# A two-layer encoder trunk with routed experts: residual inside the first expert, counts behind the selection, norm per token tile, each attention query one pair later

## The reference

```python
for l in range(2):
    sh1, sc1, g1, sh2, sc2, g2 = split(silu(c) @ w_ada[l] + b_ada[l], 6)
    h = x * (1 + sc1) + sh1
    if l == 0: y = conformer_conv(h, ...)      # 2 projections, 31 taps, norm
    else:                                      # k, v, forget gates from x;
        y = fox_attention(h @ w_q, k, v, fcum) @ w_o     # 16 heads of 64, causal
    x = layer_norm(ALPHA * x + (1 + g1) * y, ln_mix_g[l], ln_mix_b[l])
    h = x * (1 + sc2) + sh2
    probs = softmax(h @ router_w + router_b)   # group by its best two, then top 2
    y = sum over the chosen e of weight * ((silu(h @ w_gate[l,e]) * (h @ w_up[l,e])) @ w_down[l,e])
    x = layer_norm(ALPHA * x + (1 + g2) * y, ln_ffn_g[l], ln_ffn_b[l])
```

## Time and profile before

| | |
|---|---|
| timed runs | 1350.45 us median of 3 (1350.08 to 1356.78) |
| profiled execution | 1354.81 us, span 1353.1 us |
| mean granted TensorE clock | 0.923 |
| TensorE matmul | 1102.8 us busy (82%), 13118 instructions |
| VectorE, ScalarE, GpSimd | 430.4 (32%), 169.1 (12%), 21.1 us (2%) |
| DMA | 494.74 MB, mean 366 GB/s |
| chain that ended last | PE 56%, DMA 36%, DVE 4%, ACT 2%, issue 2% |

### The profile page before, as it was taken

The page is one execution under the profiler, slowest core; times in us unless marked ns, Lnnn a source line. Parts: engine busy times, 40 slices in busy tenths (PEclk is TensorE's granted clock), DMA queues, the critical chain, the costliest instruction groups (busy, mean ns, idle before and its releaser), DMA issues.

```text
span 1353.1 us, 30933 instructions
## 1 busy us (share of the span) xinstructions
PE 1102.8 (82%) x13118; PEld 653.6 (48%) x13118; DVE 430.4 (32%) x1378; ACT 169.1 (12%) x411; POOL 21.1 (2%) x61
## 2 busy tenths in 40 slices
PE   4999989669997689666999979695699996796666
PEld 2885345335554245333575853562356663453333
DVE  0697252113332123111472332431133231231114
ACT  1113130001010001000201420300010110000001
POOL 1300000000000000000000000000000000000000
PEclk9899979889999899888999989598899998998888
DMA  9985599999999999999995433789999899999990
GB/s 356 385 319 226 226 426 422 425 423 425 426 426 423 426 424 424 425 425 422 414 414 231 173 125 134 302 361 422 424 427 426 337 411 424 425 425 424 424 413 37
DMA packets 56959, 494.74 MB, mean 366 GB/s; under 512 B 4196, under 2 KB 12420, under 8 KB 17176
## 3 DMA queue, kind: packets, MB, share of 16 engines
q1 hardware_dynamic: 55920, 490.75, 87.5%
q10 hardware_dynamic: 744, 2.35, 0.5%
q0 software_dynamic: 192, 0.15, 0.0%
HBM read 492.19 MB, written 1.05 MB: 365 GB/s over the span
## 4 chain that ended last, share of the span: by engine, by line
PE 56%; DMA 36%; DVE 4%; ACT 2%; issue 2%; SPq 0%; DVEq 0%; POOLq 0%
PE PS L1079 24%; DMA ring<-in_w_up_dram 21%; DMA ring<-in_w_gate_dram 8%; PE PS L977 6%; PE PS L1201 4%; DMA ring<-in_w_down_dram 3%; PE PS L1107 3%; PE PS L884 3%; DMA work<-in_w_gate_dram 2%; PE PS L1058 2%; PE PS L994 2%; PE PS L1325 2%; DMA ring<-in_w_ada_dram 2%; PE PS L1070 1%; PE PS L1372 1%
## 5 line engine op out<-in xcount | busy, mean ns | idle before, releaser
L1079 PE MATMUL PS<-ring,work 128*32 128x256 f32 x8160 | 519.7, 411 | 171.7 <-DMA ring<-in_w_up_dram 71.6
L1079 PEld LDWEIGHTS PS<-ring,work 128*32 128x32 f32 x8160 | 282.7, 117 | 393.9 <-issue 121.2
L1641 DVE TENSOR_TENSOR work<-work,PS 128x256 f32<-128x256 f32 x47 | 19.8, 422 | 452.9 <-PE PS L1079 452.9
L977 PE MATMUL PS<-ring,work 128*128 128x512 f32 x192 | 83.4, 594 | 0.5 <-ACT work L818 0.5
L686 ACT ACTIVATE work<-PS 128x256 f32<-128x256 f32 x47 | 18.0, 383 | 449.8 <-PE PS L1079 449.8
L1079 PE MATMUL PS<-work 128*32 128x256 f32 x864 | 54.5, 394 | 16.9 <-DMA work<-in_w_gate_dram 8.5
L884 PE MATMUL PS<-ring,cact 128*32 128x512 f32 x384 | 50.3, 662 | 16.5 <-DMA ring<-in_w_ada_dram 16.5
L1201 PE MATMUL PS<-work,ring 128*128 128x256 f32 x256 | 58.1, 390 | 2.2 <-ACT work L623 2.2
L1058 PE MATMUL PS<-hs,work 128*32 128x256 f32 x784 | 56.2, 406 | 3.8 <-DVE work L1609 3.8
L1107 PE MATMUL PS<-work 32*128 32x256 f32 x784 | 56.2, 400 | 3.8 <-DVE work L1654 3.8
L977 PEld LDWEIGHTS PS<-ring,work 128*128 128x128 f32 x192 | 36.3, 190 | 46.4 <-issue 45.6
(11 more groups left out here) (254 smaller groups left out, 881.9 us busy)
## 6 DMA issues: line engine op xcount, KB each, us to landing
ring<-in_w_gate_dram SPq DMA_DIRECT2D x58, 2048.0 KB, 34.1
ring<-in_w_up_dram SPq DMA_DIRECT2D x58, 2048.0 KB, 34.9
ring<-in_w_down_dram SPq DMA_DIRECT2D x58, 2048.0 KB, 28.0
ring<-in_w_ada_dram SPq DMA_DIRECT2D x24, 2048.0 KB, 20.8
work<-in_w_up_dram SPq DMA_DIRECT2D x6, 2048.0 KB, 19.4
work<-in_w_gate_dram SPq DMA_DIRECT2D x6, 2048.0 KB, 34.1
work<-in_w_down_dram SPq DMA_DIRECT2D x6, 2048.0 KB, 42.5
ring<-in_w_pw_dram SPq DMA_DIRECT2D x8, 1024.0 KB, 12.1
```

The lines of the kernel that those rows point to most:

```text
L977: last = pe.matmul(PS[:, banks + 2 * t + q, :], moving[:, k, t * P:(t + 1) * P], quarter(index + h, kk, KH)[:, q * BANK:(q + 1) * BANK], s ...
L1079: last = pe.matmul(dst[SLOTS * s:SLOTS * (s + 1), :], rows[:, cc, SLOTS * q:SLOTS * (q + 1)], quarter(load + h, kk, KH)[:, QUART * s:QUART ...
```

## The change

- `residual` moves, in both layers, to between the hidden loop and the result loop of expert 0. `rT`'s first two chunks are scaled ahead of ScalarE's logit copy, the other six where all eight were; a Silu on one column follows them.
- In layer 0, two of the four ada loads of the K/V rows stand ahead of the counts and two behind, in PSUM bank 0 in place of bank 4.
- The mix norm: each engine normalizes its half of tile 0 and then of tile 1, with a semaphore for each tile. All transposes go tile by tile, not bank by bank.
- `hT` has a semaphore for each copying engine; the first convolution projection and the first query wait for pairs of chunks.
- The loop of pairs runs `query(i+1)` from round 1 in place of `query(i+2)` from round 0.
- The norm rows' two halves lie in different strips (partitions 72 on and 104 on), filled by eight DMAs in place of four.

```diff
+    NORM_ROWS = (NORM_ROW, NORM_ROW + 32)
-        ROWS = 16 * 7
+        ROWS = 16 * 11
             for n, w in enumerate((ln_mix_g, ln_mix_b, ln_ffn_g, ln_ffn_b)):
-                load_rows(NORM_ROW + 4 * n, w.rearrange("l (h n) -> (l h) n", n=BANK))
+                for h in range(2):
+                    load_rows(NORM_ROWS[h] + 2 * n, w[:, h * BANK:(h + 1) * BANK])
...
             def spread_ln(n, l, bank):
-                spread_row(lambda i: NORM_ROW + 4 * n + 2 * l + i, bank)
+                spread_row(lambda i: NORM_ROWS[i] + 2 * n + l, bank)
...
-                    act.activation(chunks(hs, 1)[:, 1], by_chunk(xs[:, 1, :])[:, 1], ACT.Identity, bias=negm[:, 1:2],
-                                   scale=rstd[:, 1:2]).then_inc(n_half, 1)
+                    for t in range(TT):
+                        act.activation(chunks(hs, t)[:, 1], by_chunk(xs[:, t, :])[:, 1], ACT.Identity, bias=negm[:, t:t + 1],
+                                       scale=rstd[:, t:t + 1]).then_inc(n_half, 1)
...
+                residual_T(range(2), rT_begun)
                 act.wait_ge(logits_parted, 2 * l + 1)
                 act.activation(parts[:, 0, :], PS[:, B_GATE, 0:SEQ], ACT.Copy).then_inc(parts_kept, 1)
                 act.wait_ge(lmax_ready, l + 1)
                 act.activation(r_ex[:, :, :], r_ex[:, :, :], ACT.Exp).then_inc(lexp_ready, 1)
-                for k in range(KD):
-                    last = act.activation(rT[:, k, :], ...)
-                last.then_inc(rT_ready, 1)
+                residual_T(range(2, KD), rT_ready)
+                act.activation(warm[:, :], cact[:, 0:1], ACT.Silu)
...
-                if i + Q_AHEAD < PAIRS:
-                    take_q(i + Q_AHEAD)
+                if 1 <= i < PAIRS - 1:
+                    take_q(i + 1)
...
+            def turn_h(chunk, norms=None):
+                for t in range(TT):
+                    if norms is not None:
+                        of_sums = norms % 2 == 0
+                        pe.wait_ge(h_ready, TT * (norms - 1) + (TT if of_sums else t + 1))
+                        pe.wait_ge(n_half, TT * (norms - 1) + (TT if of_sums else t + 1))
+                    for k in range(KD):
+                        last = pe.transpose(PS[:, k // 2, ...], chunk(t, k), ident[:, :])
+                        if t == TT - 1 and k % 2 == 1:
+                            last.then_inc(h_turned, 1)
-            def h_there():
-                pe.wait_ge(hT_copied, 4 * hs_turned[0])
+            def h_there(k):
+                by = (hT_by_act, hT_by_dve)[k // 2 % 2]
+                pe.wait_ge(by, 2 * hs_turned[0] - 1 + k // KH)
...
                 if l == 0:
-                    for j in range(ADA_G - 1):
-                        ada_load(L_ADAKV, j, B_GATE)
-                else:
-                    residual()
+                    pe.wait_ge(rT_begun, 1)
+                    for j in range(2):
+                        ada_load(L_ADAKV, j, 0)
...
                 if l == 0:
-                    ada_load(L_ADAKV, ADA_G - 1, B_GATE)
-                    residual()
+                    for j in range(2, ADA_G):
+                        ada_load(L_ADAKV, j, 0)
...
-                if l == 0:
-                    pe.wait_ge(ada_added, 4)
                     with pe.Fori(0, blocks):
                         hidden_of(pe.snap(n_pe) + 1, index + 6 * e)
+                    if e == 0:
+                        if l == 0:
+                            pe.wait_ge(ada_added, 4)
+                        residual()
                     with pe.Fori(0, blocks):
                         result_of(pe.snap(m_pe) + 1, index + 6 * e)
...
+                        if f == g == 0 and k % 2 == 0:
+                            h_there(k)
...
-                    dve.tensor_scalar(chunks(hs, 1)[:, 0], by_chunk(xs[:, 1, :])[:, 0], ...)
-                    dve.tensor_scalar(chunks(hs, 0), by_chunk(xs[:, 0, :]), ...).then_inc(h_ready, 1)
+                    for t in range(TT):
+                        dve.tensor_scalar(chunks(hs, t)[:, 0], by_chunk(xs[:, t, :])[:, 0], ...).then_inc(h_ready, 1)
```

More of the change, by code:

```diff
@@ L670, in moe, with residual_T @@
             def moe(l):
+                def residual_T(chunks_of, done):
+                    for k in chunks_of:
+                        last = act.activation(rT[:, k, :], PS[:, k // 2, (k % 2) * SEQ:(k % 2 + 1) * SEQ], ACT.Identity,
+                                              bias=rescol[:, 2 + l, k:k + 1], scale=rescol[:, l, k:k + 1])
+                    last.then_inc(done, 1)
+                residual_T(range(2), rT_begun)
                 act.wait_ge(logits_parted, 2 * l + 1)
@@ L818, in take_o @@
                 act.activation(QT[:, i, :], PS[:, i % 2, 0:SEQ], ACT.Copy).then_inc(o_copied, 1)
-            for i in range(Q_AHEAD):
+            for i in range(2):
                 take_q(i)
@@ L1188, in _ @@
                     for j in range(4):
-                        last = pe.matmul(PS[:, 5, 16 * j:16 * (j + 1)], rows[:, j:BANK:4], ident[:, NORM_ROW:NORM_ROW + 16],
-                                         start=True, stop=True, skip_group_check=True)
+                        of_norms = ident[:, :].rearrange("p (q r) -> p q r", q=4)[:, 2:4, NORM_ROW % 32:NORM_ROW % 32 + 8]
+                        last = pe.matmul(PS[:, 5, 16 * j:16 * (j + 1)].rearrange("p (h v) -> p h v", h=2), rows[:, j:BANK:4],
+                                         of_norms, start=True, stop=True, skip_group_check=True)
                         if j == 0:
@@ L1324, in query @@
                         arrived(L_WQ + k // KH)
+                    if i == 0 and k % 2 == 0:
+                        h_there(k)
+                        if k == 0:
+                            h_there(2)
                     last = pe.matmul(PS[:, (i + 1) % 2, SEQ:2 * SEQ],
```

62 lines of the change are left out of this document (25 added, 37 removed).

## The result

In the first comparison the changed kernel took 1340.39 us (median of 7 runs, 1338.26 to 1343.67), the kernel before beside it 1355.08 (7 runs, 1349.97 to 1356.78): ratio 0.9912, interval 0.9891 to 0.9934, which is 0.9% or 11.9 us less [8.9, 14.8]; the two medians lie 14.7 apart. A second comparison gave 1339.54 and 1355.14: 0.9885 [0.9854, 0.9915]. The time lies in the forecast's range, 2.2 us over its number. The profiled executions have spans of 1341.3 and 1341.0, against 1353.1 and, in a second profile taken later, 1356.0 before.

What follows compares the result with a forecast made beforehand. The weight stream bounds the kernel, so savings pay only before 159 us, from 631 to 883 us and in the tail. Terms -0.7 - 1.6 - 4.0 + 0.4 - 6.4 sum to -12.3: 1338.2 us from 1350.45, range 1334 to 1343.5.

Steps and rivals of the forecast that it cites:

- Per-pair waits, -0.7: First convolution projection: starting after two chunks per copying engine, 0.95 us earlier, saves 0.7 us, bounds 0.4 and 1.0.
- Strips, -1.6: Between the K halves: spread matmuls reading different row strips take 2.1 us at most, saving 1.6, bounds 1.2 and 1.8.
- Query one pair later, -4.0: Attention pair loop: query(7) fills round 6, removing a 2.67 us stall plus 1.3 of clock loss; bounds 0 and -4.4.
- Norm per token tile, +0.4: Layer 1's mix norm: scale and shift come later, so hT's copies end later, costing 0.4 us; bounds -0.2 and +1.0.
- Residual out of the routing, -6.4: Layer 1's routing: counts start at 862.5 instead of 868.87, saving 6.4 us; bounds -5.5 and -6.8.
- Residual into the first expert, 0: Layer 1's first expert: the first down slot is released later, but 3.9 us are to spare; cost 0, bounds 0 and +6.
- (1): Attention gives nothing: a softmax stall at the pair loop's head replaces the one removed at its tail; 1342.2 us, chance 0.12.
- (2): TensorE stays at half clock from the routing through layer 1's first expert, leaving 4.7 us of gain; 1345.7, chance 0.06.
- (3): The attention pair loop becomes softmax-bound in every round, losing 7.7 us overall; 1358.2 us, chance 0.03.
- (4): The start gives nothing or loses because the small norm-row DMAs land late; 1339 to 1341 us, chance 0.06.
- the forecast's tests: Wrong if the second expert stage lengthens by over 2 us, or time before 631 us changes by over 1.5.

## Why the prediction was right, and where it was off

- *The base.* The sum was -12.3 from the profiled execution, 1354.81, which gives 1342.5, and from the median shown, 1350.45, which gives 1338.2. The later medians of before are 1355.08 to 1356.33. So the three runs shown were on the fast side and the profiled one was typical; the measured differences are 11.9 (14.7 between the medians) and 15.6. The mechanism of most terms held, but that 1338.2 came within 2.2 us is partly luck: the base was 4.6 too low and the sum too small, and the two errors lie on opposite sides. From 1355.08 the same sum gives 1342.8.
- *Per-pair waits, -0.7.* The first projection starts 0.8 us sooner behind the copies (forecast 0.95). But from the third ada product to the end of "conv" almost nothing is left: with that product at full clock 128.81 before and 128.66 to 128.87 in the three kernels that had it so (query, residual and norm undone); at half clock 130.27 before and 130.19 on average in the eight with the waits per pair. Where the product was as long as before's 3.27 (3.24, both waits filled) it is 129.79, half a us less. The matmuls moved forward ran at half clock, and it came back later after the first projection: 42 to 44 us has 0.91 in before's second profile (first projection 37.90) and 0.78 in the changed kernel's first (37.46). So the edit was worth 0 to 0.5 against before, 0.1 by the mean, and not 0.7. Taking it back cost 0.6 to 1.3 in the one profile there is; that the two disagree is open. At the first query the forecast's 0 holds. The query starts 0.37 sooner (3.16 to 2.79 us from the transposes' start), but the gates' matmuls behind it now wait 0.32 for VectorE, and the second query stands 5.01 us behind the first, not 4.64. Putting the wait back costs 0.5 net (0.9 in "K/V" less 0.4 in "pairs"), more than against before, since transposing tile by tile fills the first bank later.
- *Strips, -1.6.* The spread gave 1.71. But "K/V" fell by 3.77: 0.37 is the query's wait, which "pairs" takes back, and 1.69 is the K half behind the spread, 15.70 for 14.01 in both profiles of before and never in the eleven with the fast spread. With the strips undone the clock fell elsewhere in that stage and cost 1.5. So each of the three profiles with the slow spread lost 1.5 to 1.7 us to the clock in this stage and none of the eleven others did; why, no run shows. With that the term was -3.4, about twice the forecast and outside its bounds.
- *Query one pair later, -4.0 (bounds 0 and -4.4).* "pairs" fell from 71.76 to 67.5 or 69.8: -4.3 or -1.9, and 0.37 more if the gates' wait is left out. Exactly the one wait of 2.67 went. The clock part did not come as foreseen: the fall did not go with the wait, it moved behind the next one in all nine profiles, and how long it lasts decides. Undoing the edit, with one short fall on either side, gave 3.3. That -4.0 came so near to -4.3 is luck: in both profiles of before the clock fell twice, which in the kernel with the edit undone it did not. The head of the loop had less to spare than the forecast 0.8: diagonals ready 750.42, turn at 750.64.
- *Norm per token tile, +0.4.* Undoing it gave 0.41 in its one profile, with the transposes at full clock in both (1.97 and 2.10 us). Against before's profiles it looks like -0.2, because in both of these part of the transposes was at half clock (2.65 us for 1.97).
- *Residual out of the routing, -6.4.* "wait" 6.48 to 0.05. "sums" is 10.4 in all that have no fill, as said. The forecast has no term for "select", which fell from 9.68 to 8.45 and 8.81 because the clock fell later, nor for "out", 1.0 longer in the first profile, where the clock of "pairs" was still down.
- *Residual into the first expert, 0, with 3.9 us to spare.* The cover measures 4.3 to 4.5 in the profiles, about 6 by the medians.
- *Rivals.* No stall at the head (1); the first expert rose to full clock within its hidden strips (0.71 in 870 to 874, 1.00 behind) (2); rounds 1 to 6 don't wait (3); the start didn't lose (4).

The terms as measured in the stages, -0.1 - 3.8 - 1.9 or -4.3 - 0.2 - 6.4, make -12.4 or -14.8. With "select" (-1.2, -0.9) and "out" (+1.0, 0), and without the first term, which stands earlier, these are the 12.5 and 15.5 us between 210.9 and 198.4 or 195.4. Of these some 10.4 are the waits and the spread (6.4, 2.7 and 1.7, less 0.4 in the norm). The other 2.1 or 5.1 are the clock, which stood lower in both profiles of before behind the spread, in "select" and, against the second profile of the changed kernel, in "pairs"; the forecast had 1.3 for it. Of the forecast's tests, "rest" holds. The time before 631 us holds on average: the first K matmul is at 668.32 and 669.65 before, and at 666.60 to 670.33, mean 668.4, in the eleven profiles with the first edit. In the changed kernel's own two profiles it is 1.8 and 2.0 later than in before's first, over the 1.5 allowed, and 0.5 and 0.7 later than in before's second; the stream-paced "experts 0" has two levels there, 508.0 to 508.6 and 510.5 to 510.9, that no edit here sorts. So that an edit of layer 0 gave or cost something in it can't be told.

## What to carry to other kernels

Work that depends on nothing near it goes where the bottleneck engine is waiting for data or the stream is ahead, not between a selection and its consumer; size the cover by adding work until the stage grows. Count with every slow or idle stretch of TensorE the microseconds at half clock that follow it, and compare stages only between profiles in which the clock stood alike. Take the base of a forecast from as many executions as there are: here the median of three runs was nearly 5 us off, more than any single term but one.

## What the runs showed of the chip

- Four 32-row matmuls between two strips took 1.92 us, from one strip 3.63. Only in the three profiles with the slow form did TensorE fall to 1.2 GHz in the K/V stage: in two within 8 us behind it, though it was busy throughout, and in one 45 us later.
- At the end of the first wait of 2.67 us in the pair loop, or within 2 us behind it, the granted clock fell to 0.50 in all twelve profiles with such a wait. It came back and stayed in eight, came back and fell again behind the second wait in both of before, and stayed at 0.50 through the second wait in two; in the two profiles with the waits filled it never fell.
- TensorE at half clock in the routing rose to full behind three dense matmuls (4.48 us), and after one wait of 3.77 us it was at half again.
- The third ada product, sixteen matmuls, took 1.92 us in four profiles and 3.24 to 3.64 in ten, before the change in one of each. From its start to the end of "conv" it took 128.7 to 128.9 us where it was fast and 129.8 to 131.2 where it was slow.
